# Recurrence with identity products, copied grams and tanh gates, and longer weight runs in the last expert layer

## What is computed

```python
def _rwkv_step(S, inp):
    r, w, kk, kka, kt, v = inp
    sk = jnp.einsum('bhij,bhj->bhi', S, kk)
    S = S * w[:, :, None, :] - sk[..., None] * kka[:, :, None, :] + v[..., None] * kt[:, :, None, :]
    return S, jnp.einsum('bhij,bhj->bhi', S, r)
```

## Time and profile before

| | |
|---|---|
| median of 3 timed runs | 3452.81 us (3449.86 to 3456.63) |
| the profiled execution | 3458.04 us, span of its instructions 3456.2 us |
| mean granted TensorE clock | 0.958 |
| TensorE busy | 3112.5 us, 90% |
| VectorE, ScalarE, GpSimd busy | 1644.0, 836.5, 283.2 us |
| HBM read, written | 578.50 MB, 28.44 MB |

### The profile page before, as it was taken

The page is one execution under the profiler, slowest core; times in us unless marked ns, Lnnn a source line. Parts: engine busy times, 40 slices in busy tenths (PEclk is TensorE's granted clock), DMA queues, the critical chain, the costliest instruction groups (busy, mean ns, idle before and its releaser), DMA issues. The chain is left out here.

```text
span 3456.2 us, 72498 instructions
## 1 busy us (share of the span) xinstructions
PE 3112.5 (90%) x31846; PEld 1799.8 (52%) x31846; DVE 1644.0 (48%) x3491; ACT 836.5 (24%) x1909; POOL 283.2 (8%) x297
## 2 busy tenths in 40 slices
PE   6998999989799999599999979998989878798887
PEld 5855658546344565343333335557888864232322
DVE  4574635656454586411112154238888866222211
ACT  2103410134211372100000010137766641000000
POOL 0000000000011110000000000001222230000000
PEclk9998999999899999699999989989999998899999
DMA  6564135720311223599999922100000034799998
GB/s 186 151 204 154 26 86 154 207 92 26 112 50 56 69 72 120 200 374 390 392 388 393 347 82 73 43 1 5 5 5 5 5 118 171 276 406 401 409 405 350
DMA packets 148762, 605.32 MB, mean 175 GB/s; under 512 B 17408, under 2 KB 20032, under 8 KB 131936
## 3 DMA queue, kind: packets, MB, share of 16 engines
q1 hardware_dynamic: 143424, 583.38, 45.9%
q0 software_dynamic: 5024, 17.30, 2.1%
HBM read 578.50 MB, written 28.44 MB: 176 GB/s over the span
## 5 line engine op out<-in xcount | busy, mean ns | idle before, releaser
L2126 PE MATMUL psum<-ring,big 128*32 128x256 f32 (+1 forms) x2688 | 386.5, 494 | 24.9 <-DMA ring<-moe_w 11.6
L2126 PE MATMUL psum<-front,big 128*32 128x256 f32 (+1 forms) x2384 | 320.3, 480 | 10.9 <-DMA front<-moe_w 6.4
L441 PE MATMUL psum<-h_uT,ring 128*128 128x264 f32 x1280 | 290.5, 387 | 0.0
L570 DVE SCALAR_TENSOR_TENSOR h_O<-h_O,cond_silu 128x512 f32<-128x512 f32 x336 | 227.0, 745 | 102.3 <-DMA h_O<-ada_w 102.3
L2126 PEld LDWEIGHTS psum<-ring,big 128*32 128x32 f32 (+1 forms) x2688 | 134.5, 124 | 267.2 <-issue 218.2
L441 PEld LDWEIGHTS psum<-h_uT,ring 128*128 128x128 f32 x1280 | 242.0, 190 | 46.5 <-issue 5.8
L2265 DVE TENSOR_TENSOR big<-big,psum 128x512 f32<-128x512 f32 (+1 forms) x48 | 28.7, 599 | 443.8 <-PE psum L2126 431.3
L2126 PEld LDWEIGHTS psum<-front,big 128*32 128x32 f32 (+1 forms) x2384 | 114.1, 122 | 208.8 <-issue 174.5
L2204 ACT ACTIVATE big<-psum 128x512 f32<-128x512 f32 (+1 forms) x48 | 23.5, 524 | 643.4 <-PE psum L2126 643.4
L2754 PE MATMUL psum<-ring,gates 64*64 64x128 f32 (+1 forms) x5120 | 169.4, 253 | 5.9 <-issue 4.1
L461 PE MATMUL psum<-ring,h_uT 128*128 128x512 f32 x384 | 168.3, 595 | 0.0
(11 more groups left out here) (453 smaller groups left out, 5152.4 us busy)
## 6 DMA issues: line engine op xcount, KB each, us to landing
ring<-moe_w SPq DMA_DIRECT2D x84, 2048.0 KB, 12.8
front<-moe_w SPq DMA_DIRECT2D x67, 2048.0 KB, 12.9
big<-moe_w SPq DMA_DIRECT2D x28, 2048.0 KB, 28.2
h_O<-ada_w SPq DMA_DIRECT2D x192, 256.0 KB, 2.9
ring<-w_in SPq DMA_DIRECT2D x16, 2048.0 KB, 13.1
X<-moe_w SPq DMA_DIRECT2D x13, 2048.0 KB, 12.1
ring<-na_w_qkv SPq DMA_DIRECT2D x6, 2048.0 KB, 7.9
ring<-w_out SPq DMA_DIRECT2D x4, 2048.0 KB, 9.1
```

Source lines behind the costliest of these rows:

```text
L441: last = nc.tensor.matmul(bank(k, pair_bank(q) + h, NH), w[:, a, f * P:(f + 1) * P], uT[:, a, halves[h]], start=a == 0, stop=a == KD - 1)
L570: nc.vector.scalar_tensor_tensor(into, ada(u), by, into, ALU.mult, ALU.add).then_inc(s.acc, 1)
L2126: last = nc.tensor.matmul(bank(k, b, r.width)[q * r.n:(q + 1) * r.n, :], rowsT[:, half * HALF_K + n, r.first:r.first + r.n], w[:, n, q * r ...
```

## The change

- **x in the levels.** `n_and_x` and `x_of_side` go. `raise_x` takes the place of `heads` in "up": for each of four positions, four products with M (stop=False), then four with the identity block `k.eye2` that add the old x to the x part. VectorE's `step` becomes two copies of 128x256 out of PSUM in levels 1 to 4 and one of 128x512 in levels 5 and 6.
- **Output grams.** ScalarE copies each to SBUF (`raw`), GpSimd multiplies it by its mask in place (`masked`). TensorE waits for the ScalarE copies where it waited for mask_ar and mask_br; `results` waits for GpSimd's mask_br.
- **Gates.** ScalarE computes tanh(x/2), GpSimd 0.5·t + 0.5 (`gate`).
- **bonus_sum.** Each product of 128 weight columns becomes two of 64.
- **Long runs.** In layer 1 a w2 chunk takes half the rows, four neighbouring ones per partition, so that a partition reads 16 KB in one run; `flip_hid` reads every fourth column of hid to match.

```diff
@@ expert_chunk
+    if j >= 4 and l == DEPTH - 1:
+        half = D // 2
+        return d[name][l, e, (j - 4) * half:(j - 3) * half, :].rearrange("(p a) n -> p a n", p=P)
@@ flip_hid
-                for m in range(r.width // P):
-                    at = wide(r).start + m * P
-                    last = nc.tensor.transpose(bank(k, r.ups, P, m * P), hid[:, at:at + P], k.ident[:, :])
+                blocks = r.width // P
+                mine = hid[:, wide(r)]
+                by_row = mine.rearrange("q (p m) -> q m p", m=blocks) if NS == 1 else mine.rearrange("q (m p) -> q m p", m=blocks)
+                for m in range(blocks):
+                    last = nc.tensor.transpose(bank(k, r.ups, P, m * P), by_row[:, m, :], k.ident[:, :])
@@ rwkv_scan, GpSimd
+            def gate(z, t, who, name, tile):
+                made("act", z, t, who)
+                fr["pool"][z].done(nc.gpsimd.tensor_scalar(own(tile, z), own(tile, z), 0.5, 0.5, ALU.mult, ALU.add), t, name)
+            def masked(z, t, name, tile, m):
+                after("act", z, t, f"raw_{name}")
+                shade = m[:, z, :].unsqueeze(1).to_broadcast([P, PAIRS, CH])
+                ev["pool"][z].done(tt(pairs(tile, z), pairs(tile, z), shade, ALU.mult), t, f"mask_{name}")
...
+                if m is not None:
+                    gate(y, m, "decay_tanh", "dec_gate", T_dec)
                 if f is not None:
                     rates(z, f)
-                    if lat(f):
-                        bonus_in(z, f)
+                if m is not None:
+                    gate(y, m, "iclr_tanh", "iclr_gate", T_rate)
+                if f is not None and lat(f):
+                    bonus_in(z, f)
+                if n is not None and lat(n):
+                    masked(y, n, "ar", T_ar, k.upto_less)
+                    masked(y, n, "br", T_br, k.upto_m)
@@ rwkv_scan, TensorE
+            def raise_x(z, m, with_n):
+                width = 2 * CH if with_n else CH
+                right = n_with_x(z) if with_n else x_of(z)
+                for i in range(QUAD):
+                    for b, p, flip in ((U(z), i, False), (U(z) + 1, QUAD + i, True)):
+                        pair(b, 0, p, [(m, right)], flip, stop=False, width=width)
+                    for b, p, flip in ((U(z), i, False), (U(z) + 1, QUAD + i, True)):
+                        at = p % QUAD * width + width - CH
+                        for h in range(2):
+                            lo = h * CH
+                            to = (1 - h if flip else h) * CH
+                            last = nc.tensor.matmul(bank(k, b, CH, at)[to:to + CH, :], one(lo, p), x_of(z)(lo, p), start=False, stop=True)
+                return last
...
-                made("act", z, t, "decay_gate")
+                made("pool", z, t, "dec_gate")
...
-                    last = nc.tensor.matmul(bank(k, W(z) + 1, 2, SIDE + 2 * i), own(T_dec, z)[:, i * P:(i + 1) * P], k.head_ones[:, 0:P:CH], start=True, stop=True)
+                    for g in range(2):
+                        at = i * P + g * CH
+                        last = nc.tensor.matmul(bank(k, W(z) + 1, 2, SIDE + 2 * i)[g * CH:(g + 1) * CH, :], own(T_dec, z)[:, at:at + CH],
+                                                k.head_ones[:, 0:P:CH], start=True, stop=True)
...
-                after("dve", z, t, "mask_ar" if lat(t) else "mask_m")
+                after("dve", z, t, "mask_m")
+                if lat(t):
+                    after("act", z, t, "raw_ar")
...
-                after("dve", z, t, "mask_br" if lat(t) else "mask_b")
+                after("dve", z, t, "mask_b")
+                if lat(t):
+                    after("act", z, t, "raw_br")
...
+                ev["pe"][z].done(raise_x(z, m, n < LEVELS - 1), t, f"up{n}")
@@ rwkv_scan, ScalarE
-                fr["act"][z].done(nc.scalar.activation(own(T_dec, z), own(T_dec, z), ACT.Sigmoid), t, "decay_gate")
+                fr["act"][z].done(nc.scalar.activation(own(T_dec, z), own(T_dec, z), ACT.Tanh, scale=0.5), t, "decay_tanh")
...
+            def raw(z, t, name, tile, behind):
+                after("dve", z, t, behind)
+                ev["act"][z].done(copy(groups(tile, z), woven(W(z), 1)), t, f"raw_{name}")
...
                     level(z, i, 3)
+                if n is not None and lat(n):
+                    raw(y, n, "ar", T_ar, "mask_m")
...
                 if n is not None:
+                    if lat(n):
+                        raw(y, n, "br", T_br, "mask_b")
                     rows(y, n)
                     x_first(y, n)
@@ rwkv_scan, VectorE, step
-                got = woven(U(z), 1) if n < LEVELS - 1 else side(U(z), 0)
-                x = X(z)[:, 0, :, :]
-                ev["dve"][z].done(tt(x, x, got[:, 0, :, :], ALU.add), t, f"xlow{n}")
...
-                for h in range(2):
-                    here, there = slice(h * CH, (h + 1) * CH), slice((1 - h) * CH, (2 - h) * CH)
-                    last = tt(new[there], old[here], got[there, 1, :, :], ALU.add)
-                ev["dve"][z].done(last, t, f"x{n}")
+                x = X(z)
+                if n >= LEVELS - 1:
+                    ev["dve"][z].done(nc.vector.tensor_copy(x, side(U(z), 0)), t, f"x{n}")
+                    return
+                got = woven(U(z), 1)
+                ev["dve"][z].done(nc.vector.tensor_copy(x[:, 0, :, :], got[:, 0, :, :]), t, f"xlow{n}")
+                after("act", z, t, f"Nhigh{n}")
+                ev["dve"][z].done(nc.vector.tensor_copy(x[:, 1, :, :], got[:, 1, :, :]), t, f"x{n}")
```

More of the change, by code:

```diff
@@ L2607, in scan_events @@
             + [f"up{LEVELS}"] + only("y") + ["state"],
-        act=["rows", "x0"] + [f"{x}{n}" for n in range(1, LEVELS - 1) for x in ("M", "Nhigh", "N")] + [f"M{LEVELS - 1}"],
-        dve=["mask_m"] + only("mask_ar") + ["mask_b"] + only("mask_br") + ["x0", "mask_n"] + [f"{x}{n}" for n in range(1, LEVELS + 1) for x in ("xlow", "x")]
+        act=only("raw_ar", "raw_br") + ["rows", "x0"] + [f"{x}{n}" for n in range(1, LEVELS - 1) for x in ("M", "Nhigh", "N")] + [f"M{LEVELS - 1}"],
+        dve=["mask_m", "mask_b", "x0", "mask_n"] + [f"{x}{n}" for n in range(1, LEVELS + 1) for x in (("xlow", "x") if n < LEVELS - 1 else ("x",))]
             + only("y", "y_carried") + ["state"],
-        pool=["decayed"])
+        pool=only("mask_ar", "mask_br") + ["decayed"])
     front = dict(
         pe=["dec", "iclr", "cumulate"] + only("bonus"),
-        act=["decay_gate", "iclr_gate", "d_exc", "d_inc", "d_inv"],
+        act=["decay_tanh", "iclr_tanh", "d_exc", "d_inc", "d_inv"],
         dve=["dec", "iclr", "alpha", "m", "kt", "kappa", "beta"] + only("rho", "bonus"),
-        pool=["akk"] + only("bon", "bonus_in") + ["end"])
+        pool=["dec_gate", "iclr_gate", "akk"] + only("bon", "bonus_in") + ["end"])
     return chain, front
@@ L2639, in rwkv_scan @@
     N, X = (lambda z: joint4(NX, z, 0)), (lambda z: joint4(NX, z, 1))
[L2641 to L2648, removed]
     U, W = (lambda z: 4 * z), (lambda z: 4 * z + 2)
@@ L2780, in _ @@
             n_of, x_of = (lambda z: blocks(joint(NX, z, 0))), (lambda z: blocks(joint(NX, z, 1)))
-            with_x = lambda z, other: lambda lo, p: n_and_x(z, p, other)[lo:lo + CH]
-            x_alone = lambda z, other: lambda lo, p: n_and_x(z, p, other)[lo:lo + CH, 1, :]
+            n_with_x = lambda z: both(NX, z)
+            one = lambda lo, p: k.eye2[lo:lo + CH, :]
             beta, kappa = (lambda z: woven_blocks(T_beta, z)), (lambda z: woven_blocks(T_kappa, z))
@@ L2889, in results @@
                 if lat(t):
+                    after("pool", z, t, "mask_br")
                     terms = [(rho(z), plain(T_state, z)), (plain(T_ar, z), x_of(z)), (plain(T_br, z), v_of(z, t))]
@@ L2939, in _, with decay_tanh, iclr_tanh @@
             copy = lambda out, got: nc.scalar.activation(out, got, ACT.Copy)
-            def decay_gate(z, t):
+            def decay_tanh(z, t):
                 made("dve", z, t, "dec")
-                fr["act"][z].done(nc.scalar.activation(own(T_dec, z), own(T_dec, z), ACT.Sigmoid), t, "decay_gate")
-            def iclr_gate(z, t):
+                fr["act"][z].done(nc.scalar.activation(own(T_dec, z), own(T_dec, z), ACT.Tanh, scale=0.5), t, "decay_tanh")
+            def iclr_tanh(z, t):
                 made("dve", z, t, "iclr")
-                fr["act"][z].done(nc.scalar.activation(own(T_rate, z), own(T_rate, z), ACT.Sigmoid), t, "iclr_gate")
+                fr["act"][z].done(nc.scalar.activation(own(T_rate, z), own(T_rate, z), ACT.Tanh, scale=0.5), t, "iclr_tanh")
             sums = lambda z, e: bank(k, U(z), 2 * BANK).rearrange("p (a e x) -> p a e x", e=2, x=CH)[:, :, e, :]
@@ L2987, in slot @@
                 if m is not None:
-                    decay_gate(y, m)
+                    decay_tanh(y, m)
                 if i is not None:
@@ L2991, in slot @@
                 if m is not None:
-                    iclr_gate(y, m)
+                    iclr_tanh(y, m)
                 if i is not None:
```

(8 more changed lines are left out.)

7 lines of the change are left out of this document (removed).

## The result

The changed kernel takes 3579.3 us (median of 4 runs, 3560.5 to 3586.6) where the kernel before took 3454.7 on the same chip: ratio 1.0352, 95% interval 1.0325 to 1.0378. By the ratio that is 122 us more (the medians are 125 apart), where 31 were forecast, and it lies above the range. The profiled execution has a span of 3584.8 us.

What follows compares the result with a forecast made beforehand. TensorE was taken to bound the recurrence, weight transfers layer 1's experts. Recurrence +38.5 and long runs −7.5 gave +31 us: 3489 from the profiled 3458.0, or 3484 as a timed median, 5 lower; range 3460 to 3514.

Steps and rivals of the forecast that it cites:

- part 1: Identity products raising x in the recurrence's six levels: 2.82 us more TensorE time per slot, 2.2 to 3.8.
- I take 0.47, so 2.82 us per slot: Price in us of one level's 16 identity products on TensorE, and of all six levels in a slot.
- 'issue' stays at 0.45: TensorE's idle time per full slot with no visible cause was to remain 0.45 us.
- the part on waits: TensorE's waits in the recurrence: 1.33 of 2.08 us per slot won back with results, 0.73 of 2.27 without.
- bounds of 0.36 and 0.64: Lower and upper price in us of one level's identity products in the recurrence.
- Waits for ScalarE: TensorE's 1.63 us per full slot waiting for ScalarE's copies, expected mostly covered by the identity products.
- Parts 2 and 4: Recurrence: output grams moved to ScalarE and GpSimd cost nothing; split bonus sum saves 0.25 us per slot with results.
- Part 3: Tanh gates in the recurrence: both table loads go, ScalarE falls to 11.8 us per slot, GpSimd's extra operations cost nothing.
- Part 5: Long w2 runs in layer 1's experts: 0.5 us saved per expert, −7.5 us in all (−5 to −10).
- The rivals: Recurrence: sets hidden, 3444 (0.08); table loads stay, 3497 (0.07); GpSimd late, 3526 (0.05). Experts: long runs worth more, 3470 (0.05).

Runs made afterwards that it cites:

- e2: Kernel before plus 16 products of one weight column by one moving column ahead of each level's x product, which overwrites them; ratio 1.0400.
- e8: Kernel before plus 96 one-column products per step, all bunched ahead of level 1's x product; ratio 1.0612.
- e11: Kernel before plus 16 one-column products at levels 1, 3 and 5 alone; ratio 1.0207.
- e12: Kernel before plus 96 products per step of 64 weight by 64 moving columns, all bunched ahead of level 1's x product; ratio 1.0378.
- e1: Changed kernel without the identity products and copies of x, VectorE's old sums back; ratio 1.0002 to the kernel before.
- e10: Kernel before with only the long runs and the tanh gates; ratio 0.9964.
- e6: Kernel before with only the long runs of layer 1's w2 and the matching order of hid's blocks; ratio 0.9982.
- e4: Kernel before with the 16 key-rate products of 64 weight columns written as 8 of 128; ratio 1.0054.

## Why the prediction was wrong

- **Direction, place and part were right**: a loss, in the recurrence, from the identity sets; TensorE as the engine that sets the time, though by the supply of its instructions and not by its work.
- **The step that failed** is the price in part 1, "I take 0.47, so 2.82 us per slot", with "'issue' stays at 0.45" in the part on waits. 0.47 was read from neighbouring starts in short stretches, and so were its bounds of 0.36 and 0.64. Over a whole slot the measured price is 5.3 to 5.7 us for six sets, 0.9 each. At 69 records per us the added 400 give 5.8 in a slot with results, and e2, e8, e11 and e12 show that the count sets it. The sign was there to be read: two windows of very different content had the same records per us, and that quotient was not formed. The range failed with it, as all its ends came from short stretches.
- **Waits for ScalarE**: right that they end (forecast 1.33 of 1.63 us for ScalarE won back, measured nearly all), wrong that this is a gain. TensorE now stands 3.9 us per slot for its next instructions, more than the 2.1 that it idled before.
- **Parts 2 and 4, output grams and bonus sum at about nothing**: right that no wait for the raw copies appears and that the bonus sum keeps TensorE busy for less (9.0 us in fourteen slots instead of 14.7, 0.4 per slot). Wrong that both together gain a little: e1 against e10 shows a loss of some 13 us. **Part 3**: right. No table load stands in the slots, ScalarE has 12.2 us per slot (11.8 forecast), GpSimd 9.4 (10 to 12); the gates take 0.62 us, not 1.0 to 1.8. The loads of before take 1.28 us, with 0.02 idle ahead of each and 0.01 between one and its exponential, so what went is the 2.6 us of the rows and not 5.3.
- **VectorE** has 14.2 us per slot, 13.4 forecast. The copies cost what was said; one product of the front (`beta`, L3093) takes 0.5 us more than before:

```profile
L3135 DVE COPY ring<-psum 128x256 f32<-128x256 f32 x56 | 23.8, 425 | 74.9 <-PE psum L2793 74.9
...
L3132 DVE COPY ring<-psum 128x512 f32<-128x512 f32 x28 | 19.4, 692 | 49.8 <-PE psum L2793 49.8
L3093 DVE TENSOR_TENSOR ring<-ring 128x512 f32<-128x512 f32 x14 | 16.8, 1203 | 0.0
```

- **Part 5**: -7.5 forecast, -4.2 in the trace of the changed kernel, -6 by e6: right in size. Over 400 us of the experts the rate is 406 GB/s before, 410 in the changed kernel and 414 in e6. The change keeps this gain, and it hides part of the loss.
- **The rivals**: none came. Those on the recurrence varied which wait ends last; none asked whether TensorE could be fed at the new rate.

That supply is the limit is shown by the stops inside the bunches, where nothing else can be waited for; that these are the packets' arrivals is shown by their times: all 85 stops of the changed kernel, and the 42 and 48 in e8 and e12, end 1.19 to 1.62 us behind a packet's end. The period of 3.7 us is then made up of three times in the changed kernel: a packet moves for 1.07 us (mean), TensorE goes on 1.38 later (median), and the next packet starts 1.16 after that (median, never under 1.04), 3.6 us together. Open is why these follow one another instead of overlapping; no run changed them.

## What to carry to other kernels

Count TensorE's records per us over whole slots before pricing an added product. Where unlike stretches share one quotient, here 66 to 70, suspect that the engine is at its supply of instructions; "issue" stops that end a fixed time behind the instruction packets show it. There an added product costs by its number, not by its columns, and waits seen on other engines are cover that is not to be had. Put such work into few wide products, or leave it on an engine with room; and a set timed between two neighbouring starts tells only what it costs while instructions are at hand.

## What was not expected of the hardware

- **Supply of instructions**: 69 to 70 products and loads per us at most over a stretch (e2, first window), 256 per 16 KB packet; in bursts 32 records of products with their loads in 0.47 us. The Trainium skill (Runtime: NRT & Kernel Launch, "Instruction fetch mechanics") says that an engine's instructions are fetched in blocks of 16 KiB, 256 instructions, ahead of their use, and that crossing a block's end is mostly hidden. The block agrees; hidden it is not here: "issue" is 3.9 us of a 27.25 us slot.
- **The clock** was lower where products of one column stood in a bunch: 0.81 and 0.84 in e8's slots without and with results, and 1.00 with 64 columns in the same places (e12). Spread over the levels they left it at 0.99 in e2's slots without results and 0.90 in those with them.
- **Merging quadrants** can cost: 16 records of 64 rows by 128 weight columns, all in one half of the rows, took 1.92 us, twice the 29 to 32 records of 64 by 64 that they replaced (e4).
- **VectorE beside GpSimd**: `beta` above has a mean of 1203 ns, and 692 in before. Eleven of its fourteen instances lie 0.5 us or more beside a mask on GpSimd and take 1.05 to 1.49 us; the other three lie 0.07 us or less beside one and take 0.68. In e10, which has no masks on GpSimd, `kappa` and `beta` have 693.

```profile
L3062 DVE TENSOR_TENSOR ring<-ring 128x512 f32<-128x512 f32 x14 | 9.7, 693 | 1.5
L3067 DVE TENSOR_TENSOR ring<-ring 128x512 f32<-128x512 f32 x13 | 9.0, 693 | 0.4
```
